# A hybrid attention, Hyena and expert layer: the output product moved in between attention's steps

## The reference, cut to what matters

```
h = rms_norm(x) * (1 + sc1) + sh1
q, k, v, hy = split(h @ w_in)
att = attend(q, k, v)                    # 8 heads of 64; softmax
hyo = hyena_mixer(hy)                    # long convolution
merged = concat[rms_norm(att) * gnorm_att, rms_norm(hyo) * gnorm_hyena]
x  = x + gt1 * (merged @ w_out)          # the output product
h2 = rms_norm(x) * (1 + sc2) + sh2
x  = x + gt2 * hier_moe(h2)              # top-1 group, top-2 of its 4 experts, 16 experts in all
y  = rms_norm(x) * final_g
```

## Time and profile before

| | us |
|---|---|
| median of 3 runs | 850.86 |
| lowest and highest | 848.81 and 852.36 |
| the profiled execution's own time | 853.53 |
| its span in the profile | 851.8 |
| PE busy (share of the span) | 720.0 (85%) |
| DVE, ACT, GpSimd busy | 531.4, 398.1, 172.2 |

### The profile page before, as it was taken

One profiled execution on the slowest core, in us unless ns is written; L12 is line 12 of the kernel. 1 busy time (PEld: TensorE's weight loads), 2 busy tenths in 40 slices (PEclk: granted clock), 3 DMA queues, 4 the chain that ended last, 5 costly groups with the idle time before them and its releaser, 6 DMA issues. The chain is left out here.

```text
span 851.8 us, 10418 instructions
## 1 busy us (share of the span) xinstructions
PE 720.0 (85%) x3772; PEld 547.7 (64%) x3772; DVE 531.4 (62%) x793; ACT 398.1 (47%) x592; POOL 172.2 (20%) x170
## 2 busy tenths in 40 slices
PE   2798999899999968879997379999999998989800
PEld 1247998759898646634455368877777777778600
DVE  3546416476512158834333659898999899989638
ACT  1455333410322147720112157777767776777433
POOL 2000000000121058304331300333322233221000
PEclk9999999999999969969997589999999999999965
DMA  9990135220495390000105973999999999998263
GB/s 331 408 376 2 67 132 199 98 95 18 141 230 236 111 384 2 2 0 1 49 25 211 399 266 97 372 380 360 344 360 366 357 362 345 354 366 318 79 251 136
DMA packets 67197, 183.75 MB, mean 216 GB/s; under 512 B 4593, under 2 KB 4625, under 8 KB 63825
## 3 DMA queue, kind: packets, MB, share of 16 engines
q1 hardware_dynamic: 58080, 161.39, 51.0%
q0 software_dynamic: 7312, 19.61, 6.5%
q10 hardware_dynamic: 1760, 2.17, 0.9%
HBM read 175.26 MB, written 14.19 MB: 222 GB/s over the span
## 5 line engine op out<-in xcount | busy, mean ns | idle before, releaser
L1338 DVE TENSOR_TENSOR WL<-slot,WH 128x1024 fp32r<-128x1024 f32 x192 | 222.0, 1220 | 1.3 <-ACT WH L903 0.9
L903 ACT CAST WH<-slot 128x1024 fp32r<-128x1024 f32 x192 | 187.1, 1053 | 21.7 <-DMA slot<-in_w_up 15.7
L1536 PE MATMUL bank<-WH,xgTh 128*128 128x512 f32 x256 | 104.8, 409 | 19.5 <-DVE WL L1338 18.1
L1536 PE MATMUL bank<-WL,xgTh 128*128 128x512 f32 x256 | 101.8, 398 | 0.0
L1536 PE MATMUL bank<-hTh,WP 128*128 128x384 f32 (+1 forms) x320 | 99.6, 311 | 2.6 <-DVE hTl L1054 2.4
L1536 PE MATMUL bank<-WH,xgTl 128*128 128x512 f32 x256 | 101.7, 397 | 0.0
L1536 PE MATMUL bank<-hTl,WP 128*128 128x384 f32 (+1 forms) x320 | 98.8, 309 | 0.0
L1536 PE MATMUL bank<-hTh,WL 128*128 128x384 f32 (+1 forms) x320 | 98.8, 309 | 0.0
L662 POOL DMA_INDIRECT y_scratch<-big x16 | 67.3, 4206 | 110.9 <-DVE big L1371 110.9
L1441 PE MATMUL bank<-slot,big 128*128 128x512 f32 (+1 forms) x224 | 86.6, 547 | 0.0
L1450 PE MATMUL bank<-ident,big 128*128 128x128 f32 x424 | 63.6, 292 | 13.3 <-DMA big<-h_scratch,big 8.6
(11 more groups left out here) (227 smaller groups left out, 1061.7 us busy)
## 6 DMA issues: line engine op xcount, KB each, us to landing
slot<-in_w_gate SPq DMA_DIRECT2D x16, 2048.0 KB, 14.0
slot<-in_w_up SPq DMA_DIRECT2D x16, 2048.0 KB, 20.0
slot<-in_w_down SPq DMA_DIRECT2D x16, 2048.0 KB, 9.3
slot<-in_w_ada SPq DMA_DIRECT2D x12, 2048.0 KB, 11.6
slot<-in_w_in SPq DMA_DIRECT2D x6, 2048.0 KB, 11.7
big<-in_x SPq DMA_DIRECT2D x2, 2560.0 KB, 23.3
big<-y_scratch SPq DMA_DIRECT2D x5, 1024.0 KB, 8.9
slot<-in_w_out SPq DMA_DIRECT2D x2, 2048.0 KB, 10.6
```

Source lines behind the costliest of these rows:

```text
L903: act.copy(WH[:, high_half(w, s), r, :], quarter(s, w, r)).then_inc(high_ok[w], 1)
L1338: dve.tensor_tensor(WL[3 * s + w][:, r, :], quarter(s, w, r), WH[:, high_half(w, s), r, :].bitcast(F32), ALU.subtract).then_inc(low_ok[w], 1)
L1536: ins = pe.matmul(out, l[u], r[v], start=first and i == 0, stop=last and i == 2)
```

## The change

The separate stage of the output product is gone. A table FILL says which groups of it PE does in which step of attention, between the scores of v+1 and the values of v-1; the loops of all engines now run to step 28. Only tile 4's attention half (`wa`, 4, n) lies behind the last step, in steps 21 and 22. DVE no longer joins the two halves: each group is scaled by its norm's factor and gt1 in one operation (`weighted`) and added to x on its own by GpSimd, and for the last two groups by DVE. That makes 20 additions where there were 10 multiplications and 10 additions. The roots of attention's norm and of h2's norm are taken per tile, inside the steps. The root of Hyena's norm, and the wait for gt1, stand ahead of the first step.

The scores use two banks in place of four. GpSimd issues gt1's loads when K is done, ahead of V, and those of G2 and SH2 in step 1. SP issues x between the two chunks of w_out. The first expert's gate and up weights go to slots 1 and 2 after the last group of the product; its down weights go to slot 0, which attention's probabilities use, and wait for the last tile's routing product (`rt`), and the second expert's six megabytes wait behind them and for the stores of h2. h2T has one buffer in place of two.

```diff
+STEPS = PAIRS * NT + 9
+FILL = {2: [("wh", 0, 0)], 3: [("wh", 1, 0)], 4: [("wh", 2, 0)], 5: [("wh", 3, 0)], 6: [("wh", 0, 1)],
+        7: [("wa", 0, 0)], 8: [("wa", 0, 1)], 9: [("wh", 1, 1)], 10: [("wh", 2, 1)], 11: [("wa", 1, 0)],
+        12: [("wa", 1, 1), ("h2", 0)], 13: [("wh", 3, 1)], 14: [("wh", 4, 0)], 15: [("wa", 2, 0)],
+        16: [("wa", 2, 1), ("h2", 1)], 17: [("wh", 4, 1)], 19: [("wa", 3, 0)], 20: [("wa", 3, 1), ("h2", 2)],
+        21: [("wa", 4, 0)], 22: [("wa", 4, 1), ("h2", 3)], 28: [("h2", 4)]}
...
-                add(("s", u), "dve", u % 4)
+                add(("s", u), "dve", u % 2)
...
             sp.dma_start(x, a["x"].rearrange("(t p) n -> p t n", p=P)).then_inc(in_x, 16)
+            load_chunk(NCH - 1)
...
             full(sp, *LAST_JOB[-1])
-            load_expert(0, 0)
-            sp.wait_ge(h2_ok, NT)
+            load_expert(0, 0, rest=lambda: full(sp, "rt", NT - 1))
+            sp.wait_ge(h2_out[0], 16 * 3)
+            sp.wait_ge(h2_out[1], 16 * 2)
             load_expert(1, 1)
...
+            for u in range(3):
+                bias(u)
+            have(pool, "kp", 1)
+            pool.wait_ge(m_out[0], 64)
+            for c in range(2):
+                rows_of(gt1[:, c, :], c, 2, gt1_in)
+            for v in range(-1, STEPS):
+                if v == 1:
+                    have(pool, "V", NT - 1)
+                    pool.wait_ge(m_out[1], 64)
+                    for c in range(2):
+                        rows_of(G2[:, c, :], c, 4, g2_in)
+                        rows_of(SH2[c], c, 3, sh2_in)
+                for f in FILL.get(v - 1, ()):
+                    if f[0] != "h2" and ADDED[f] <= len(SUMS) - 2:
+                        add_up(f)
+                for u in heads(v + 2) if v >= 0 else (3,):
+                    if u < CT * H:
+                        bias(u)
...
+                if stat_of(v) is not None:
+                    have(act, "ast", b)
+                    act.activation(ss[:, 4, b:b + 1], ss[:, 3, b:b + 1], ACT.Sqrt, scale=1.0 / CH, bias=epsb[:, :])\
+                        .then_inc(att_rt, 1)
+                if v > PAIRS and v % PAIRS == 2 and 0 <= b - 1 < NT:
+                    act.wait_ge(x1_sq, b)
+                    act.activation(ss[:, 1, b - 1:b], ss[:, 0, b - 1:b], ACT.Sqrt, bias=epsb[:, :]).then_inc(n_rt, 1)
...
+            def weighted(f):
...
+                drain(dve.scalar_tensor_tensor(out=w, in0=bk[:, :], scalar=rsh[:, 1 if kind == "wh" else 0, b:b + 1],
+                                               in1=gt1[:, b // CT, cols], op0=ALU.mult, op1=ALU.mult), *f)
+                if i > len(SUMS) - 2:
+                    have(dve, *f)
+                    dve.wait_ge(wt2_ok, len(SUMS) - 2)
+                    dve.tensor_tensor(x[:, b, cols], x[:, b, cols], w, ALU.add).then_inc(x1_ok, 1)
...
+            for v in range(-1, STEPS):
+                if v + 1 < PAIRS * NT:
+                    scores(v + 1)
+                if stat_of(v) is not None:
+                    att_stat(stat_of(v))
+                for f in FILL.get(v, ()):
+                    if f[0] == "h2":
+                        route(f[1])
+                    else:
+                        mixed(f)
+                if 1 <= v <= PAIRS * NT:
+                    values(v - 1)
+                if 0 <= v < PAIRS * NT:
+                    for u in heads(v):
+                        turn_probs(u)
```

More of the change, by code:

```diff
@@ L168 @@
 ORD = {}
+LATER = {("ast", NT - 1): ("wa", NT - 1, 0)}
 for _name, _bank, _eng in JOBS:
-    ORD[_name] = 1 + sum(1 for n in ORD if JOBS[JOB[n]][2] == _eng)
+    if _name not in LATER.values():
+        for _n in (_name, LATER.get(_name)):
+            if _n is not None:
+                ORD[_n] = 1 + sum(1 for n in ORD if JOBS[JOB[n]][2] == _eng)
 LOADS = [(("ada", 0, 0), 0), (("ada", 0, 1), 1), (("ada", 0, 2), 2), (("win", WVH), 0), (("ada", 0, 3), 3),
@@ L475, in turned_h2 @@
                 bk = full(act, "h2T", b, g)
-                if b >= 2:
-                    full(act, "rt", b - 2)
-                drain(act.copy(h2T[:, b % 2, 4 * g:4 * g + 4, :].rearrange("p a b -> p (a b)"), bk[:, :]), "h2T", b, g)
+                if b >= 1:
+                    full(act, "rt", b - 1)
+                drain(act.copy(h2T[:, 4 * g:4 * g + 4, :].rearrange("p a b -> p (a b)"), bk[:, :]), "h2T", b, g)
         def chunk_src(c):
@@ L519, in _ @@
             sp.dma_start(x, a["x"].rearrange("(t p) n -> p t n", p=P)).then_inc(in_x, 16)
-            for i in range(2, NCH):
+            for i in range(2, NCH - 1):
                 load_chunk(i)
@@ L531, in load_expert @@
                         sp.wait_ge(used[j], ended * 4)
+                    if j == 2 and rest is not None:
+                        rest()
                     src = w[bass.ds(e, 1), :, :] if not isinstance(e, int) else w[e:e + 1, :, :]
@@ L868, in att_squares, with x1_square @@
                 act.activation(osq, oraw[:, b % 2], ACT.Square).then_inc(osq_ok, 1)
-            for v in range(-1, PAIRS * NT):
+            def x1_square(b):
+                act.wait_ge(wt2_ok, ADDED[("wa", b, 1)] if b < NT - 1 else len(SUMS) - 2)
+                if b == NT - 1:
+                    act.wait_ge(x1_ok, 2)
+                if b >= 2:
+                    full(act, "h2T", b - 2, 1)
+                    act.wait_ge(h2_out[b % 2], 16 * (b // 2))
+                act.activation(h2[:, b % 2, :], x[:, b, :], ACT.Square, scale=1.0 / 32.0,
+                               accum_out=ss[:, 0, b:b + 1]).then_inc(x1_sq, 1)
+            act.wait_ge(hrt, 1)
+            act.activation(ss[:, 6, :], ss[:, 5, :], ACT.Sqrt, scale=1.0 / CH, bias=epsb[:, :]).then_inc(hy_rt, 1)
+            for v in range(-1, STEPS):
                 if v + 1 < PAIRS * NT:
@@ new lines, in _ @@
+            dve.wait_ge(hy_rt, 1)
+            link(dve.reciprocal(rsh[:, 1, :], ss[:, 6, :]))
+            dve.wait_ge(gt1_in, 32)
+            dve.wait_ge(in_small, 80)
+            for v in range(-1, STEPS):
+                if v + 1 < PAIRS * NT:
+                    for u in heads(v + 1):
+                        scores(u)
+                b = v // PAIRS - 1
+                if stat_of(v) is not None:
+                    stat(b)
+                if v + 1 < PAIRS * NT:
+                    for u in heads(v + 1):
+                        normed(u)
+                if stat_of(v) is not None:
+                    dve.wait_ge(att_rt, b + 1)
+                    link(dve.reciprocal(rsh[:, 0, b:b + 1], ss[:, 4, b:b + 1]))
+                if v > PAIRS and v % PAIRS == 1 and b < NT:
+                    out_sums(b)
+                if v > PAIRS and v % PAIRS == 2 and 0 <= b - 1 < NT:
+                    if b == 1:
+                        dve.wait_ge(g2_in, 32)
+                        dve.wait_ge(sh2_in, 32)
+                    modulated(b - 1)
+                for f in fillers_out(v):
+                    if f[0] == "h2":
+                        logits(f[1])
+                    else:
+                        weighted(f)
+                if 1 <= v <= PAIRS * NT and v % PAIRS == 0:
+                    out_tile(b)
@@ L1681, in att_stat @@
                 close(pe.matmul(bk[:, b:b + 1], osum[:, b % 2, :], ones[:, 0:1], start=True, stop=True))
-            for v in range(-1, PAIRS * NT + 1):
-                if v + 1 < PAIRS * NT:
-                    scores(v + 1)
-                if v >= 1:
-                    values(v - 1)
-                if v > PAIRS and v % PAIRS == 2:
-                    att_stat(v // PAIRS - 1)
-                if 0 <= v < PAIRS * NT:
-                    for u in heads(v):
-                        turn_probs(u)
-            att_stat(NT - 1)
-            Ws = [chunk(("wout", n)).rearrange("p (k n) -> p k n", n=512) for n in range(2)]
-            pe.wait_ge(hg_ok, CB)
-            pe.wait_ge(att_ok, NT)
             def route(b):
```

213 lines of the change are left out of this document (85 added, 128 removed).

## The result

| | before | changed |
|---|---|---|
| median of the runs, us | 851.5 (848.81 to 852.36) | 837.14 (836.18 to 840.37) |
| profiled execution: its time / its span, us | 853.5 / 851.8 | 836.18 / 834.4 |

The ratio of the runs is 0.9837, with a 95% interval of 0.9814 to 0.9861: 14 us faster, 12 to 16 by the interval. The forecast was 833 us and a gain of 17.7 us. 837.14 lies inside the range of 828 to 843, and just above the 829 to 837 of its main case. The two profiled executions lie 17.4 us apart. But the changed one was the fastest of its four, and the one before (853.5) lies above all four of its runs, so of this agreement with 17.7 some 3 us are luck.

The account below looks back on a forecast made before the run. It took PE to bound attention and the output product, with pauses of 15.0 us and lowered clock in attention. Logits 19.2 us earlier, gather +1.0, start +0.5 make -17.7; 850.9 - 17.7 gives 833 us, range 828 to 843.

Parts of the forecast that it names:

- main case: Whole kernel: the prediction's own forecast of 829 to 837 us, given a chance of 0.62.
- Attention with 18 groups: From PE's first transposes at 300 us: own work, groups, three routings, clock and pauses end the last values product at 428.6 us.
- the pauses that stay: PE's waits left in attention's steps: bounded between 1 us less than none and 13 us more, taken as 2 us.
- The tail: From the last values product's end (t0) through DVE, ACT and PE to the last logits: t0 + 22.6 us.
- The logits: Last tile's logits done at 451.2 us where they were done at 470.4, 19.2 us earlier.
- the start's 0.5: Before the first scores DVE waits for the root of Hyena's norm: 0 to 2 us, taken as 0.5 us.
- The gather: First expert's gather, issued amid that expert's weight loads: 0 to 3.8 us later, taken as 1 us.
- The experts' stage: Experts' products after the logits: as long as before, 320 us.
- Pauses stay in the steps: Attention steps: table loads (7.7 us) or group waits (up to 13 us) reach PE, 837 to 846 us; chance 0.20.
- Bias tiles still stall attention: Early attention: GpSimd's late bias tiles still stall DVE and PE; if all stays, 838 us; chance 0.06.
- GpSimd the bound: Attention steps: additions ahead of bias tiles slow GpSimd; at 8 us a step, 858 us; chance 0.05.
- More is gained: Attention and tail: no pauses stay and the tail's products run at full clock, 828 us; chance 0.07.

Follow-up runs that it names:

- warm_tail: Changed kernel with one hidden-part group of the last tile moved from an attention step to the first step behind the last values product: 836.27 us, ratio 0.9822.
- routing_split: Changed kernel with each routing taken apart: transposes behind their step's values products, 20-column products at the head of the next step's filler: 824.81 us, ratio 0.9718.
- split_tail: Changed kernel with routings taken apart and, on DVE, tile 3's logits added behind tile 4's modulation: 826.55 us, ratio 0.9730.
- before_mods_later: Kernel before with only the six loads of modulation rows issued after the eighth head's bias tile, not the fourth's: 844.11 us, ratio 0.9937.
- mods_together: Changed kernel with GpSimd issuing all six loads of modulation rows together in step 0, as the kernel before does: 842.86 us, ratio 0.9922.
- pool_extra: Changed kernel with one more 128x512 multiplication by ones on GpSimd ahead of each of its 18 additions: 835.72 us, ratio 0.9830.
- tables_extra: Changed kernel with one more exponential and square root behind each tile's attention root, ten more table loads on ACT: 844.83 us, ratio 0.9917.

## Why the prediction was right, and where its terms were off

**The bound and the mechanism.** Right: PE's pauses ahead of the last values product were the thing to win, and a group in each step wins them: where PE paused for 15.0 of 71.7 us, it is busy 97% of the time from 307 to 428.6 us, at the clock of 1.00 that was forecast but for the places of the routings.

**Attention with 18 groups, forecast 128.6 us to the end of the last values product.** Measured from T 128.6 and 129.0 in the two profiles of the changed kernel, and yet not by the terms as written. In the first of them: a group cost 3.63 and not 3.50 us: +2.4 us in all. A routing cost 4.23 (twice) and 4.73 and not 3.57 us: +2.5 us. The value came from the output product, where the bank for the second transposes had long been emptied; the new place has a wait of 0.41 us more and a clock that falls. The rest, attention's own work with its half-clock start and the pauses that stay, was 50.1 and not 49.8 + 3.2 + 2.0 = 55.0 us. That is below even the lower end of the bound (no pauses and 1 us less: 52.0). One part of it is the start: half clock was over 4.3 us after T, where six transposes take 0.88 us (at 306.30), and not after 6.5. The errors cancelled, which is luck.

**The tail, forecast 22.6 us.** Measured 26.0, and this is the step that failed. Two terms of it make up 3.2 of the 3.4 us: the group behind t0 was put at 3.5 us and took 5.37, at lowered clock, though the same text let PE stand there for 1.5 us and took half clock for the products at the end; and DVE's h2 of tile 4 was not held against DVE's own order, where tile 3's logits stand ahead (1.3 us). The order was there to be read. What lowers the clock at the first is open: warm_tail filled the pause, and the group still took 5.40 us; with the third routing moved it took 3.68 in routing_split and 5.24 in split_tail, in the same order.

**The logits.** Forecast 18.7 us earlier (with the start's 0.5), measured 13.8: 3.4 us of the difference are the tail; 1.6 us lie ahead of attention, where the program is unchanged (the modulation's last product begins at 291.70 against 290.11 us; in the second profile of the changed kernel it was 288.34). That part is scatter. The start itself cost 0.44 us, as forecast.

**The gather.** Forecast 1 us later, measured 0.65 us earlier, logits to first product. It waited under the loads no longer than before. The term was small and its sign wrong: 1.65 us between forecast and measurement.

**The experts' stage.** Forecast unchanged, measured 315.0 against 317.6 us. A gain of 2.6 us that no step of the prediction had, and the reason why the profiled pair comes out at 17.4 us.

**The rivals.** *Pauses stay in the steps* did not come, in any row of a long step; that 837.14 us touches its 837 to 846 comes from the tail. *Bias tiles still stall attention* did not either: DVE's wait of 3.40 us is left, longer than the 1 us that the prediction's signs allowed, but under a group; what that part is worth is shown both ways, 5.4 us added alone (before_mods_later) and 8 us taken away by the medians (mods_together). *GpSimd the bound*: refuted by pool_extra. *More is gained* did not come, as the tail kept its pause and its low clock. routing_split goes past that rival's 828 us (824.81 us, 0.9718 of the kernel before), by the routings, which the rival did not name.

**The rules weighed.** The Trainium skill (ScalarE: Activation LUTs, What ACT_TABLE_LOAD costs) would have the six added switches cost an estimated 16 us of ACT. Here a load row is 1.28 us, the instruction behind it starts within 0.02 us (361.14 + 1.28, next row 362.43), and in long steps four extra ones cost the kernel nothing. Its advice to do all functions of one set before switching (same page, Table sets: the hidden batching unit) holds here for places without cover, as tables_extra shows. The shared port of VectorE and GpSimd (SBUF — State Buffer, Who interferes with whom) changed no total: pool_extra's addition took 1.60 us beside DVE's work in the step shown, where 1.27 is its mean in the changed kernel and 1.29 in pool_extra, and it was hidden.

## What to carry over

A product that needs nothing fills the pauses of a loop of short dependent products nearly for its bare cost, and in a long step its place hardly matters; what matters is that every step has one (warm_tail took one out and saved nothing) and that nothing on the helper's queue stands ahead of what the loop needs next. Then look at the steps that break the pattern: here taking a routing apart gave 1.5 to 2.9 us, with two waits of about half a us gone and no lowered clock behind it, while the steps around it lost nothing. And in a tail of single instructions go through each engine's own order, not only through the chain of data.

## What the runs showed of the chip that I had not expected

The granted clock fell where PE had been busy most of the time. Around a routing with waits of 0.41 and 0.68 us, in the second profile of the changed kernel:

```profile
404.00:409.00 5.00, 4.40 (x35) 3.70 (x36) 1.70 (x6) 1.03 (x3) 0.56 (x1) 0.85 0.00 0
409.00:414.00 5.00, 5.00 (x14) 1.83 (x12) 2.38 (x11) 2.44 (x7) 0.00 (x0) 0.81 0.00 2
```

PE is busy 4.40 of 5 us and then all of 5 us, and the clock is 0.85 and 0.81: part of each stretch runs at the lower level of 1.2 GHz, and the group in it lasts 4.89 us. The same place of the same program kept 2.4 GHz in another execution, so the routing does not bring the clock down every time; why it falls is open. Some of the scatter between executions may come from there; that was not tried.
